# Retrieval stage of a decoder layer: one combined u/v fetch per pick, against u by pick and v by token

## The reference

```python
def block(tb):
    ...
    idx = jnp.take_along_axis(cand_i, pos, axis=-1)
    gate = jax.nn.softmax(best_s, axis=-1).astype(tb.dtype)
    act = jax.nn.gelu(jnp.einsum('thkd,td->thk', peer_u[idx], tb), approximate=False)
    return jnp.einsum('thk,thkd->td', gate * act, peer_v[idx])
```

## Time and profile before

| | us |
|---|---|
| median of three runs (6094.88 to 6118.96) | 6117.32 |
| profiled execution | 6114.73 |
| its span (first to last recorded instruction) | 6112.9 |
| busy PE / DVE / POOL / ACT in the span | 4892.2 / 3182.6 / 1747.7 / 861.3 |
| PEER, from the first fetch | 3004.32 to the end |

### The profile page before, as it was taken

How to read it: one execution, slowest core, us unless ns; L and a number is a source line. 1 busy time by engine, 2 the same in 40 slices (tenths; PEclk the granted TensorE clock), 3 DMA queues, 4 the chain that set the end, 5 groups by cost and what they waited for, 6 DMA issues and landing times.

```text
span 6112.9 us, 54374 instructions
## 1 busy us (share of the span) xinstructions
PE 4892.2 (80%) x19251; PEld 2961.5 (48%) x19251; DVE 3182.6 (52%) x7617; ACT 861.3 (14%) x1824; POOL 1747.7 (29%) x1329
## 2 busy tenths in 40 slices
PE   5999999978885848679477777877777777777999
PEld 3777777765565837479333233333333333332222
DVE  2444444425453121221585857677676868585443
ACT  2232223213222121110000000000000000000000
POOL 0111111101011221122154544444444545454221
PEclk8999999979997979889799999999999999999555
DMA  1000010001113023202499999999999999999664
GB/s 61 26 25 25 27 38 25 12 33 36 36 43 134 28 76 112 98 28 91 167 419 421 408 418 410 413 413 410 407 416 412 412 414 409 412 418 383 155 153 114
DMA packets 226760, 1304.74 MB, mean 213 GB/s; under 512 B 30832, under 2 KB 60272, under 8 KB 82480
## 3 DMA queue, kind: packets, MB, share of 16 engines
q0 software_dynamic: 157696, 1140.92, 47.5%
q1 hardware_dynamic: 68912, 161.99, 7.5%
HBM read 1263.52 MB, written 39.29 MB: 213 GB/s over the span
## 4 chain that ended last, share of the span: by engine, by line
DMA 24%; PE 15%; DVE 9%; issue 3%; ACT 1%; POOL 0%; SPq 0%; DVEq 0%
DMA peer_rows<-in_peer_uv,peer_picked_index 23%; PE psum_bank L1911 13%; DVE peer_rows L2129 3%; DVE peer_diagonal L2140 2%; PE psum_bank L1892 1%; PE psum_bank L1874 1%; DVE peer_top_index L1995 0%; DVE peer_position L1988 0%; DVE peer_sums_left L1989 0%; DVE peer_position L1995 0%; DVE peer_sums L2084 0%; DVE peer_best L1985 0%; DVE peer_best L1992 0%; ACT peer_scores L1939 0%; POOL peer_rows L1863 0%
## 5 line engine op out<-in xcount | busy, mean ns | idle before, releaser
L1911 PE MATMUL psum_bank<-peer_rows,peer_diagonal 128*128 128x512 f32 (+1 forms) x4608 | 2370.2, 667 | 612.0 <-DVE peer_diagonal L2140 611.1
L1911 PEld LDWEIGHTS psum_bank<-peer_rows,peer_diagonal 128*128 128x128 f32 (+1 forms) x4608 | 877.4, 198 | 2080.7 <-issue 1105.2
L1863 POOL DMA_INDIRECT peer_rows<-in_peer_uv,peer_picked_index x1152 | 1341.1, 1164 | 1817.7 <-PE psum_bank L1911 1674.5
L2129 DVE SCALAR_TENSOR_TENSOR peer_rows<-peer_rows,peer_tokens 128x1024 f32<-128x1024 f32 (+1 forms) x1152 | 1390.9, 1220 | 620.3 <-DMA peer_rows<-in_peer_uv,peer_picked_index 619.8
L445 PE MATMUL psum_bank<-x_normed,dn_weights 128*128 128x384 f32 (+1 forms) x1536 | 529.4, 488 | 13.0 <-DMA dn_conv_w<-in_dn_conv_w 13.0
L1958 ACT ACTIVATE peer_gelu<-peer_dots 128x2 f32<-128x2 f32 (+1 forms) x576 | 116.4, 203 | 2791.7 <-DVE peer_rows L2129 2791.5
L2140 DVE TENSOR_SCALAR peer_diagonal<-const_ident,peer_gelu,peer_picked_gates 128x128 f32<-128x128 f32 (+1 forms) x1152 | 340.6, 337 | 249.1 <-PE psum_bank L1911 247.7
L753 POOL TENSOR_TENSOR dn_block<-dn_lower,dn_level_masks 128x1152 f32<-128x1152 f32 x56 | 146.8, 2628 | 1004.1 <-DVE dn_lower L831 890.4
L445 PEld LDWEIGHTS psum_bank<-x_normed,dn_weights 128*128 128x128 f32 x1536 | 287.9, 198 | 154.4 <-issue 23.0
L1023 PE MATMUL psum_bank<-x_normed,ssd_w_xz 128*128 128x384 f32 (+1 forms) x768 | 249.3, 485 | 3.1 <-ACT ssd_b_tokens L1152 3.1
L1023 PEld LDWEIGHTS psum_bank<-x_normed,ssd_w_xz 128*128 128x128 f32 x768 | 150.9, 199 | 92.8 <-issue 12.2
(11 more groups left out here) (419 smaller groups left out, 6043.3 us busy)
## 6 DMA issues: line engine op xcount, KB each, us to landing
peer_rows<-in_peer_uv,peer_picked_index POOLq DMA_INDIRECT x1152, 15.8
dn_weights<-in_w_dn SPq DMA_DIRECT2D x8, 2048.0 KB, 7.2
retrieval_q<-w_pq_stage SPq DMA_DIRECT2D x16, 576.0 KB, 2.8
peer_q<-retrieval_q SPq DMA_DIRECT2D x9, 1024.0 KB, 47.8
heads<-mixed_heads SPq DMA_DIRECT2D x16, 544.0 KB, 9.2
ssd_w_xz<-in_w_xz SPq DMA_DIRECT2D x8, 1024.0 KB, 4.7
cache_k<-in_cache_k SPq DMA_DIRECT2D x8, 1024.0 KB, 6.3
cache_v<-in_cache_v SPq DMA_DIRECT2D x8, 1024.0 KB, 8.0
```

What stands on the lines that cost most here:

```text
L1863: nc.gpsimd.indirect_dma_start(out=uv[0:n, m % RING, :], out_offset=None, in_=d["peer_uv"], in_offset=bass.IndirectOffsetOnAxis(ap=index[0 ...
L1911: mm = nc.tensor.matmul(ACC[half_][0:n, :], diag[0:n, m % TURNED, 0:n], uv[0:n, m % RING, D_MODEL + 512 * half_:D_MODEL + 512 * half_ + 51 ...
L2129: op = nc.vector.scalar_tensor_tensor(uv[0:n, m % RING, 0:D_MODEL], uv[0:n, m % RING, 0:D_MODEL], 1.0, x[0:n, i % 2, :], ALU.mult, ALU.mul ...
```

## The change

u and v become two arrays of 4 KB rows. u is fetched as before, one indirect DMA per pick for 128 tokens, into a ring of 8 slots that DVE alone frees. v is fetched token by token: one indirect DMA brings the 128 picks of one token, so the picks lie in the partitions. For that the index table is turned by PE (`PICKS_T`) and cast (`index_t`). The weights, gelu times gate, are made once per tile when all dots are there (one gelu, one product), and turned by PE (`WEIGHTS_T`). PE then sums a token's 128 v rows by a product with a block of 32 columns that is zero but for the token's column of weights: ACT copies that column into the middle of a zero block (`shifts`), and PE reads the block from a shifted place. A group g is four tokens, g, 32+g, 64+g and 96+g, whose results go to four strips of 32 partitions of the same banks. The sum of tile i-1 runs beside the dots of tile i, so the loops have one more round, and the end of a tile moves one round later.

```diff
-    RING, PAIR, TURNED = 11, 2, 4
+    URING, PAIR, STRIPS, HELD, SHIFTS = 8, 2, 4, 3, 4
+    GROUPS = P // STRIPS
+    strips_of = lambda i: STRIPS if i < LAST else SAMPLE // GROUPS
...
-        diag = sb("diagonal", [P, TURNED, P])
-        uv = sb("rows", [P, RING, 2 * D_MODEL])
+        shifts = sb("shifted_weights", [P, STRIPS, SHIFTS, 2 * GROUPS])
+        u, w = sb("u_rows", [P, URING, D_MODEL]), sb("v_rows", [P, HELD, STRIPS, D_MODEL])
...
             @block.gpsimd
...
+                def fetch_u(i, k):
+                    m = SLOTS * i + k
+                    n = rows_of(i)
+                    if k == 0:
+                        pool.wait_ge(index_ready.sem, index_ready.at(i + 1))
+                    if m >= URING and m % PAIR == 0:
+                        pool.wait_ge(dotted.sem, dotted.at((m - URING) // PAIR + 1))
+                    nc.gpsimd.indirect_dma_start(
+                        out=u[0:n, m % URING, :], out_offset=None, in_=d["u_rows"],
+                        in_offset=bass.IndirectOffsetOnAxis(ap=index[0:n, i % 2, k:k + 1], axis=0)).then_inc(u_fetched[m % URING].sem, 16)
+
+                def fetch_v(i, g, b):
+                    m = GROUPS * i + g
+                    if g == 0 and b == 0:
+                        pool.wait_ge(index_t_ready.sem, index_t_ready.at(i + 1))
+                    if m >= HELD and b == 0:
+                        pool.wait_ge(used.sem, used.at(m - HELD + 1))
+                    t = GROUPS * b + g
+                    nc.gpsimd.indirect_dma_start(
+                        out=w[:, m % HELD, b, :], out_offset=None, in_=d["v_rows"],
+                        in_offset=bass.IndirectOffsetOnAxis(ap=index_t[:, i % 3, t:t + 1], axis=0)).then_inc(v_fetched[m % HELD][b].sem, 16)
+                nc.gpsimd.memset(shifts[:, :, :, :], 0.0).then_inc(blanked.sem, 1)
+                for i in range(NC + 1):
+                    for g in range(GROUPS):
+                        for b in range(STRIPS):
+                            if i < NC:
+                                fetch_u(i, STRIPS * g + b)
+                            if i and b < strips_of(i - 1):
+                                fetch_v(i - 1, g, b)
...
                     mm.then_inc(summed.sem, 1)
+                    pe.wait_ge(index_ready.sem, index_ready.at(i + 1))
+                    nc.tensor.transpose(PICKS_T, index_f[:, :], const["ident"][:, :]).then_inc(picks_turned.sem, 1)
...
                 def weigh(i, g):
...
+                    m = GROUPS * i + g
+                    pe.wait_ge(shift_ready.sem, shift_ready.at(m + 1))
+                    for b in range(strips_of(i)):
+                        sig = v_fetched[m % HELD][b]
...
+                        pe.wait_ge(sig.sem, sig.at(loads))
+                    for half_ in range(2):
+                        for b in range(strips_of(i)):
+                            mm = nc.tensor.matmul(ACC[half_][GROUPS * b:GROUPS * b + GROUPS, :],
+                                                  shifts[:, b, m % SHIFTS, GROUPS - 1 - g:2 * GROUPS - 1 - g],
+                                                  w[:, m % HELD, b, 512 * half_:512 * half_ + 512],
+                                                  start=False, stop=(g == GROUPS - 1))
+                    mm.then_inc(used.sem, 1)
...
-                for i in range(NC):
-                    residual(i)
+                for i in range(NC + 1):
+                    if i:
+                        residual(i - 1)
+                        turn_weights(i - 1)
...
-                        weigh(i, g)
+                        if i and g % 2:
+                            weigh(i - 1, g // 2)
...
             @block.scalar
...
+                def make_gelu(i):
+                    n = rows_of(i)
+                    act.wait_ge(dotted.sem, dotted.at(STEPS_PER_TILE * i + STEPS_PER_TILE))
+                    if i:
+                        act.wait_ge(weight_turned.sem, weight_turned.at(i))
+                    nc.scalar.activation(weight[0:n, :], dots[0:n, :], ACT.Gelu).then_inc(gate_used.sem, 1)
...
             @block.vector
...
+                    settle(nc.vector.scalar_tensor_tensor(index_f[:, :], SUMS[:, 0:P], float(NK), column[:, :], ALU.mult, ALU.add))
+                    v.wait_ge(vec.sem, vec.now())
+                    nc.vector.tensor_copy(index[:, i % 2, :], index_f[:, :]).then_inc(index_ready.sem, 1)
...
-                        op = nc.vector.scalar_tensor_tensor(uv[0:n, m % RING, 0:D_MODEL], uv[0:n, m % RING, 0:D_MODEL], 1.0, x[0:n, i % 2, :],
-                                                            ALU.mult, ALU.mult, accum_out=dots[0:n, i % 2, k:k + 1])
+                        op = nc.vector.scalar_tensor_tensor(u[0:n, m % URING, :], u[0:n, m % URING, :], 1.0, x[0:n, i % 2, :],
+                                                            ALU.mult, ALU.mult, accum_out=dots[0:n, k:k + 1])
...
-                def make_diagonal(i, g):
+                def make_weights(i):
                     n = rows_of(i)
...
+                    v.wait_ge(gate_used.sem, gate_used.at(i + 1))
+                    nc.vector.tensor_tensor(weight[0:n, :], weight[0:n, :], gate[0:n, i % 2, :], ALU.mult).then_inc(weight_ready.sem, 1)
```

More of the change, by code:

```diff
@@ L1847, in _ @@
                         load_q(i + 1)
-                    if i:
-                        store(i - 1)
+                    if i > 1:
+                        store(i - 2)
+                store(LAST - 1)
                 store(LAST)
@@ L1903, in residual, with turn_weights @@
                                          start=(k % 4 == 0), stop=False)
+                def turn_weights(i):
+                    pe.wait_ge(weight_ready.sem, weight_ready.at(i + 1))
+                    nc.tensor.transpose(WEIGHTS_T, weight[:, :], const["ident"][:, :]).then_inc(weight_turned.sem, 1)
                 def weigh(i, g):
[L1906 to L1914, removed]
+                    m = GROUPS * i + g
+                    pe.wait_ge(shift_ready.sem, shift_ready.at(m + 1))
+                    for b in range(strips_of(i)):
+                        sig = v_fetched[m % HELD][b]
+                        loads = m // HELD + 1
+                        if i == LAST and b >= strips_of(LAST):
+                            continue
+                        pe.wait_ge(sig.sem, sig.at(loads))
[6 more added lines that the diff above has]
+                    mm.then_inc(used.sem, 1)
                 pe.wait_ge(once.sem, once.at(3))
@@ L1948, in root, with make_shift @@
                     nc.scalar.activation(norm[:, :], norm[:, :], ACT.Sqrt).then_inc(root_ready.sem, 1)
+                def make_gelu(i):
[4 more added lines that the diff above has]
+                    nc.scalar.activation(weight[0:n, :], dots[0:n, :], ACT.Gelu).then_inc(gate_used.sem, 1)
+                def make_shift(i, g):
+                    m = GROUPS * i + g
+                    if g == 0:
+                        act.wait_ge(weight_turned.sem, weight_turned.at(i + 1))
+                    if m >= SHIFTS:
+                        act.wait_ge(used.sem, used.at(m - SHIFTS + 1))
+                    n = strips_of(i)
+                    nc.scalar.activation(shifts[:, 0:n, m % SHIFTS, GROUPS - 1:GROUPS],
+                                         WEIGHTS_T.rearrange("p (b m) -> p b m", m=GROUPS)[:, 0:n, g:g + 1], ACT.Copy).then_inc(shift_ready.sem, 1)
                 take_scores(0)
                 exp(0)
-                for i in range(NC):
-                    n = rows_of(i)
+                act.wait_ge(blanked.sem, 1)
+                for i in range(NC + 1):
                     for g in range(STEPS_PER_TILE):
[L1955 to L1958, removed]
+                        if i and g % 2 == 0:
+                            make_shift(i - 1, g // 2)
                         if i < LAST and g == SCORES_AT:
@@ L1962, in _ @@
                             exp(i + 1)
-                        if i and g == 1:
-                            root(i - 1)
+                        if i > 1 and g == 1:
+                            root(i - 2)
+                    if i < NC:
+                        make_gelu(i)
                 root(LAST)
```

64 lines of the change are left out of this document (31 added, 33 removed).

## The result

The changed kernel takes 6199.31 us (median of four runs, 6184.79 to 6224.58) against 6117.27 for the kernel before in the same comparison: ratio 1.0147, interval 1.0106 to 1.0188, so 1.1 to 1.9% slower. The forecast was 6425 us: the right sign and inside its range, but the loss was overstated, 5.0% in place of 1.5.

What follows compares the result with a forecast made beforehand. Before, transfers bound eight full tiles and PE the ninth; after, POOL's fetches would set the full tiles' pace. 3005 + 235 + 2688 + 371 + 124 = 6423 us of span, time 6425 us; range 6060 to 6640 us.

Steps and rivals of the forecast that it cites:

- start: Before the first tile's u: an extra copy, transpose and cast cost 1 us, so u starts near 3005.
- stage 0: u of tile 0 alone, with the search of tile 1: DVE is the bound, 235 us, between 205 and 260.
- stages 1 to 7: u of one full tile beside v of the tile before: POOL sets the pace, 7 x 384 = 2688 us.
- stage 8: u of the last 64 tokens and v of tile 7: 256 fetches, no search, 2.9 us per pair, 371 us.
- the end: v of the last tile: 64 fetches without dots, turning weights before and 9 us behind, together 124 us.
- 0.25 us of hold per fetch, hence 3.0 us per pair: Full tiles: dots delay each POOL fetch by 0.25 us, so one u and one v fetch take 3.0 us.
- locked pattern: Full tiles: a dot holds a fetch that ends two pairs after the first, 2.76 us per pair; not expected to hold.
- The first rival: Full tiles: dots fall between fetches, DMA binds at 2.56 us per pair, time 5987 us; chance 0.23.
- Landings that move: Full tiles: argument against dots falling between fetches, landing times shift, with only 0.02 us of room per pair.
- The wait at a tile's end: Each tile waits for dots, gelu, turned weights and first shift; covered by fetches, some 10 us per tile if uncovered.
- second rival: v products on PE run at the lower clock: 13.6 us per group, tiles of 447 us, 6981 in all; chance 0.05.
- The lock on both sides: First stage: by the port rule fetches would hold dots too, about 0.47 us each, 60 us more than the sum.

## Why the prediction was right or wrong

**Sum.** The terms of the forecast, measured: start 3011.6 for 3005 (+7; the first fetch was 2 us later, and its landing was counted in stage 0), stage 0 216 for 235 (-19), stages 1 to 7 2441 for 2688 (-247), stage 8 429 for 371 (+58), the end 126 for 124 (+2): 6423 - 199 = 6224, against a span of 6222.8.

**The sign was right in part by luck.** The forecast put the loss into the eight stages of the full tiles (235 + 2688 for 2636 us, +287) and little of it behind them (371 + 124 for 473, +22). The runs have it the other way round: +20 and +82.

**The step that failed: 0.25 us of hold per fetch, hence 3.0 us per pair.** That POOL would become the party that waits for nothing, held up by dots, was right (groups after; tokens in PSUM). The size was not: 0.12 us and 2.72, so that stages 1 to 7 took 2441 us for 2688. The 0.25 of the earlier trace rows came from a kernel in which POOL waits for slots, so that a fetch begins when PE has freed one, and it was carried over as if it were a property of a fetch. The prediction had DMA at 2.56 us and POOL at 2.48 side by side and treated them as separate limits; being 3% apart, they are coupled through the landing times, and the coupling picks the harmless place (theory E). Where DMA is taken out of play, the forecast's 3.0 is nearly met: 2.93 us with half of v, 2.89 (2589 / 896) with seven eighths. The prediction's "locked pattern" of 2.76 us comes closest by number, but by another way: it has a hold of 0.28 per pair from an unloaded DMA, which the run with half of v doesn't show. It also has u landing 3.5 us after its issue; in 4300 to 4620 us of the changed kernel the median is 6.5 (issues, us to landing):

```profile
peer_u_rows<-in_u_rows,peer_picked_index POOLq DMA_INDIRECT x117, 6.5
```

**The first rival**, dots between the fetches, holds for part of the time: 2.61 to 2.71 us per pair in the steps without search, 2.72 to 2.83 in those with. Its signs came, too: a fetch mean near 1.0 us (1.056) and a DMA share of 1.0 (1.01). "Landings that move", the argument against it, was half right: the search moves the dots, the load on DMA brings them back.

**Stage 8: costed by the wrong resource.** It was taken as 256 fetches of POOL at 2.9 us per pair. DMA bound it, at 235 GB/s and 3.35 us per pair. That DMA goes slower into 64 partitions than into 128 was in the earlier trace rows: 143 GB/s at a DMA share of 0.63 in the last tile are 227 at a full share, against 412 / 1.01 in the full tiles. The prediction read only the 0.90 us of issue there. By that row alone, u at 227 and v at 408 GB/s would make 1.15 + 1.28 = 2.4 us per pair, still under POOL's 2.9; the stage went as if v, too, ran at u's rate. The packets show that it did: from 5750 to 6050 us a packet of 4 KB took 285 ns on average and 99 in 100 took over 228, though two thirds of them are v's. With u for 128 partitions they took 163 (5700 to 5950 us of that run). Why v's packets slow down as well is open. The Trainium skill (SBUF — State Buffer, section "Door 1: The DMA port swizzle") says that partitions 0 to 63 reach only 8 of 16 ports and gives about 218 GB/s as the most for them. The 227 GB/s of the earlier trace rows agree in direction, and no run here shows ports.

**Stage 0** came within its bounds (216 us in 205 to 260). **The end** is 2 us off, but by luck: from 6110 to 6200 us v landed after 5.4 us (median), not 3.5, and PE took 1.91 us for 25 of the 32 groups of two strips, not 3.4. The forecast's own terms there, 2.48 + 3.5 + 3.4, make 9.4 us and not 9.8. **The wait at a tile's end** (gelu, turned weights) doesn't show in the stages, as forecast.

**PE.** Right that it is covered, wrong in how. A group of the changed kernel (start, us, idle before it):

```profile
4196.68 3.64 PE L1949 MATMUL psum_bank<-peer_v_rows,peer_shifted_weights 128*32 128x512 f32 x16 [7.64 <-DMA peer_v_rows<-in_v_rows,peer_picked_index_t]
```

The granted clock in these 3.64 us is 0.50. The 6.8 us of the forecast were for 16 instructions one after another at 1.00, those of the second rival, 13.6, for the same at 0.50, so the strips run side by side. The granted clock is 0.62 on average in stages 1 to 7, so for the most part the lower of its two levels, 1.2 GHz, after stretches in which PE waited for v (it is busy 898 of 2441 us, 37% for the forecast's 55 to 65); it is not the 1.00 of the earlier trace rows. The second rival's lower clock came about, its price didn't: a group is fed in 4 x 2.72 = 10.9 us.

**DMA's share** was forecast near 0.85 at 350 GB/s, and is 1.01 at 389. Seen alone it names DMA as the bound. But POOL never waits for a slot, and with tokens in PSUM DMA moved 404 GB/s: it came near that only in the steps without search, with 390 to 403 GB/s from tile to tile, against 377 to 387 in those with. POOL was forecast to be busy for over 90%; its own fetches of 1.2 us with 0.30 between them make 80%, and 78 was measured (1894 of 2441 us).

**The lock on both sides**, by the rule of the Trainium skill (SBUF — State Buffer, section "SBUF: two separate sides") that the prediction weighs, isn't seen on the dots: they last 1.22 us in all these kernels, though in the changed one 114 start less than 0.2 us into a fetch. Only the fetch is held.

## What to carry to other kernels

A stall measured where its engine has slack is no price for the day it becomes the bound; take its range, and ask which party will set the rhythm. Where two parties are within a few per cent of each other, their phase adjusts, and taking load off the one that seemed to bind can make the kernel slower. Cost a moved transfer on DMA as well as on its issuer, by GB/s over DMA share of the nearest row with as many partitions. Where transfers of different widths share the engines, even that can be too low (2.4 us here, 3.35 measured): such a mix is to be measured.

## What was unexpected

- Less data made it slower: 128 columns of v less, 6199 to 6319 us.
- One operand of the dots in PSUM frees the fetches wholly (0.00 to 0.01 us held wherever the dot starts), at 1.220 us per dot against 1.223.
- DMA shares of 1.01 to 1.03 stood beside 389, 393, 404 and 408 GB/s in streams of 4 KB rows; a share of one doesn't say that no more would go.
- A stream of 64 and 128 partitions in turn ran at 235 GB/s, while the same bytes into 128 ran at 404.
